# Projections and attention in one stage: tiles in three rounds, gates last, first maxima between the last gate tiles

## The chip, the cores and the metric

The kernel runs on one core of one Trainium2 chip. Times are microseconds on the device. The core has five engines with a queue each: PE (TensorE, matmuls; PEld its weight loads), DVE (VectorE), ACT (ScalarE), POOL (GpSimd) and SP (SyncE, which here only issues DMAs). They wait for each other by semaphores alone. The metric is the device time of one execution, given as the median of several.

## What is computed

Two residual blocks follow each other on 2048 tokens of width 1024: gated linear attention, then a block with attention and a convolution side by side. The change lies in the second.

```python
u = rms_norm(h, norm_w) * (1.0 + scale) + shift
p = u @ w_in                                   # 1024 -> 2816 columns
q, k, v = qk_heads(p, q_norm_w, k_norm_w)      # 8 query heads, 2 key heads, width 64
q = rope_2d(q, angles)
k = rope_2d(k, angles)
k_c, v_c = kv_heads(uc @ w_in[:, K_LO:V_HI], k_norm_w)     # 256 context keys
k_all = jnp.concatenate([k_c, k], axis=1)      # 2304 keys
v_all = jnp.concatenate([v_c, v], axis=1)
attn = attend_blocked(q, k_all, v_all) * jax.nn.silu(p[..., ZA_LO:ZA_HI])
conv = conformer_conv(p[..., GLU_LO:GLU_HI], ...) * jax.nn.silu(p[..., ZC_LO:ZC_HI])
out = jnp.concatenate([attn, conv], axis=-1) @ w_out
h = h + gate[:, None, :] * out
```

`attend_blocked` is a softmax over all 2304 keys for each query head. `conformer_conv` is a gated input, a depthwise convolution of 31 taps over the tokens, a layer norm, a swish and a pointwise product.

## The kernel before

Everything is float32; a product is made of three passes with the operands split into a high and a low part. The second block has three stages, each with its own buffers and with a barrier of all engines ahead of it (L1256, L1837, L2295): `projections`, `attention`, `output`. The first two belong to different phases, so the SBUF of `projections` is given back before that of `attention` is taken.

**Projections** (L1147). The 2048 tokens are four blocks of 512. For each block b, `NW = 22` tiles of 128 output columns are made, j = 0 to 21, block after block: 88 tiles, each 24 matmuls (L1421) into one of two banks, G[j % 2]. Tiles 0 to 7 are the convolution's input and its gate in turn, 8 to 12 the four pairs of query heads and the keys, 13 the values, 14 to 21 the eight gates `za` and `zc`. ACT reads a tile out of its bank (L1554 to L1576; a gate tile is read twice, once plain and once through a tanh), and the next but one tile may then be written. DVE makes from two reads the convolution's input (L1658) or a gate (L1709), which SP stores. What is kept between ACT and DVE lies in `ga` and `gt`, two slots each.

The heads go through a chain spread over the following tiles: squares summed over a head by PE (L1430), a root by ACT and DVE, spread back by PE (L1436), scaled by DVE (L1686), halves swapped by eight small DMAs of SP (`swap_q`, L1285), turned by DVE (`turn_q`, `add_turned_q`) and stored by SP to the scratch tensors `qt` and `kt` (`store_q`, L1291). In block b the chain ends in the first tile of block b + 1; the last block's ends after its last tile.

The convolution's 4 x 124 taps (each a multiply and add over 512 or, in the last block, 528 tokens, `tap`, L1618) run on DVE behind what each tile needs of it; `OWN` says how many go with each tile. What is left of a block's taps after its last tile runs with the first four tiles of the next.

**Attention** (L1732). 32 steps, one for each query head and block of 512 queries, eight heads over two groups of keys (g = 0, 1). A step has 18 key tiles, kt. For each: scores of 128 keys x 512 queries into one of three banks `att_bank_s` (L1970, L1971), an exponential by ACT (L2070) into `p_f`, and the sum of `p_f` pair by pair (POOL L1915, DVE L2135). The product with the values (`weigh`, L1945) comes in three groups of twelve matmuls, two in the step (at kt 9 and 14) and one in the next (at kt 2).

The exponential needs a row of maxima first, one value for each query, subtracted within the scores through row 65 of `q_b`. These maxima are taken one step ahead: 20 pieces (`piece`, L1930) of raw scores, 4 at a time between the key tiles of the step before, in four banks `att_bank_m`; DVE reduces each piece (L2121); after the last a small reduction (L2127), a transposition by PE (L1937) and a read by ACT (L2023) give the row. From the fifth piece on, PE waits before a pair of pieces for the reductions that free its banks:

```python
if p % 2 == 0:
    need(pe, mx_read, i * NP + max(p - MBANKS + 2, 0))
```

Step 0 has no step before it. Its pieces stand by themselves at the head of the stage, after the loads of Q and K (SP L1846, L1857), the rounding of K to its high part by ACT (`round_k`, L2012) and of Q (L2019). POOL makes the low part of K (L1901), 64 x 2304 values in one instruction, for each group. SP also loads V (L1861).

## Time and profile before

| | us |
|---|---|
| median of 3 runs (lowest, highest) | 2650.35 (2646.22, 2656.89) |
| the profiled execution, whole | 2648.54 |
| its span | 2646.5 |
| PE busy | 2470.5 (93%) |
| DVE busy | 1687.6 (64%) |
| ACT busy | 1008.9 (38%) |
| POOL busy | 694.6 (26%) |
| mean granted PE clock | 0.971 |

PE is the engine on the path nearly everywhere. The projections run from 1044.3 to 1574.3, the attention from there to about 2370, the output to the end. In the page's row of forty slices the granted clock stands at 0.8 to 0.9 of full speed except in one slice, the 25th, where it is 0.6: that slice holds the seam between projections and attention. A share of 1.00 is the full clock of 2.4 GHz, 0.50 is 1.2 GHz. The profiled execution lies between the lowest and the median run.

### The profile page before, as it was taken

The page shows a single profiled execution, that of the slowest core. Times are in us where ns is not written, and L with a number is a line of the kernel's source. Part 1 is how long each engine was busy: PE and PEld are TensorE (multiplying, and loading weights), DVE is VectorE, ACT ScalarE, POOL GpSimd, SP SyncE. Part 2 cuts the span into 40 slices and gives each one's busy share as a digit, 9 for nine tenths or more (in the row PEclk, how much of TensorE's full clock was granted, in tenths as well). Part 3 has the DMA queues.
Part 4 walks back from the last instruction along what each step waited for, and adds up shares of the span by engine and source line. Part 5 has one row for each costly group of instructions (what it writes and reads, how often), then busy time and mean ns, then how long its engine had stood idle before and what let it go on. Part 6 is the DMA issues. An engine that isn't in the chain of part 4 may idle for free. (4 is left out here: it accounts for less than half of the span.)

```text
span 2646.5 us, 33253 instructions
## 1 busy us (share of the span) xinstructions
PE 2470.5 (93%) x11265; PEld 1698.2 (64%) x11265; DVE 1687.6 (64%) x2746; ACT 1008.9 (38%) x1766; POOL 694.6 (26%) x313
## 2 busy tenths in 40 slices
PE   3898899999999998999999976999999999988997
PEld 1576677777777777777777763554555445546776
DVE  3236564654656461889997984777777777775664
ACT  4144444444345440332222123555445445451222
POOL 1233211111211100102000003677666566640000
PEclk8999999999999999999999996999999999998999
DMA  7964787388668747488767654111111110104334
GB/s 269 358 201 141 245 289 279 132 278 318 210 220 282 275 150 271 174 283 318 236 224 240 213 177 104 49 49 54 31 31 29 30 30 25 27 25 169 131 136 153
DMA packets 225145, 453.62 MB, mean 171 GB/s; under 512 B 23957, under 2 KB 82571, under 8 KB 224756
## 3 DMA queue, kind: packets, MB, share of 16 engines
q1 hardware_dynamic: 193960, 351.04, 39.3%
q10 hardware_dynamic: 31052, 100.87, 11.1%
q8 instruction: 76, 1.25, 0.2%
q14 instruction: 57, 0.47, 0.1%
HBM read 328.86 MB, written 109.35 MB: 166 GB/s over the span
## 5 line engine op out<-in xcount | busy, mean ns | idle before, releaser
L2121 DVE TENSOR_REDUCE att_mx<-att_bank_m 128x1 f32<-128x512 f32 (+1 forms) x640 | 365.2, 629 | 128.9 <-PE att_bank_m L1930 128.9
L2070 ACT ACTIVATE att_p_f<-att_bank_s 128x512 f32<-128x512 f32 x576 | 312.4, 599 | 284.1 <-PE att_bank_s L1971 276.0
L1915 POOL TENSOR_TENSOR att_den<-att_den,att_p_f 128x1024 f32<-128x1024 f32 x160 | 379.4, 2371 | 42.7 <-ACT att_p_f L2070 27.4
L1618 DVE SCALAR_TENSOR_TENSOR proj_conv_acc<-proj_conv_in,proj_conv_w,proj_conv_acc 128x512 f32<-128x512 f32 (+1 forms) x480 | 337.4, 772 | 0.0
L562 PE MATMUL gla_bank_g<-mid_a_hi,mid_w_hi 128*128 128x512 f32 x768 | 310.8, 405 | 2.0 <-POOL mid_w_lo L515 1.1
L562 PE MATMUL gla_bank_g<-mid_a_hi,mid_w_lo 128*128 128x512 f32 x768 | 300.8, 392 | 0.0
L562 PE MATMUL gla_bank_g<-mid_a_lo,mid_w_hi 128*128 128x512 f32 x768 | 300.1, 391 | 0.0
L1945 PE MATMUL att_bank_o<-att_p_f,att_v 128*64 128x512 f32 x1152 | 270.6, 605 | 0.0
L562 PEld LDWEIGHTS gla_bank_g<-mid_a_hi,mid_w_hi 128*128 128x128 f32 x768 | 144.9, 189 | 48.3 <-issue 18.5
L1945 PEld LDWEIGHTS att_bank_o<-att_p_f,att_v 128*64 128x64 f32 x1152 | 74.6, 137 | 146.0 <-issue 104.9
L562 PEld LDWEIGHTS gla_bank_g<-mid_a_hi,mid_w_lo 128*128 128x128 f32 x768 | 144.6, 188 | 31.5
L562 PEld LDWEIGHTS gla_bank_g<-mid_a_lo,mid_w_hi 128*128 128x128 f32 x768 | 145.0, 189 | 29.4 <-issue 1.4
L508 POOL TENSOR_TENSOR mid_w_lo<-first_w_raw,mid_w_hi 128x1024 fp32r<-128x1024 f32 x22 | 54.7, 2486 | 379.6 <-ACT mid_w_hi L736 379.6
L1421 PE MATMUL proj_bank_g<-mid_a_hi,mid_w_hi 128*128 128x512 f32 x352 | 140.5, 399 | 5.7 <-PEq L1256 5.7
L1421 PE MATMUL proj_bank_g<-proj_u_hi,mid_w_hi 128*128 128x512 f32 x352 | 139.5, 396 | 0.0
L1421 PE MATMUL proj_bank_g<-mid_a_lo,mid_w_hi 128*128 128x512 f32 x352 | 137.6, 391 | 0.0
L1421 PE MATMUL proj_bank_g<-mid_a_hi,mid_w_lo 128*128 128x512 f32 x352 | 137.5, 391 | 0.0
L1421 PE MATMUL proj_bank_g<-proj_u_lo,mid_w_hi 128*128 128x512 f32 x352 | 137.1, 389 | 0.0
L1421 PE MATMUL proj_bank_g<-proj_u_hi,mid_w_lo 128*128 128x512 f32 x352 | 136.9, 389 | 0.0
L1970 PE MATMUL att_bank_s<-att_q_a,end_k_a 128*128 128x512 f32 x288 | 130.6, 454 | 1.0 <-ACT att_q_b L2023 1.0
L1970 PE MATMUL att_bank_s<-att_q_a,att_k_a 128*128 128x512 f32 x288 | 128.8, 447 | 2.4 <-issue 2.0
L1915 POOL TENSOR_TENSOR att_den<-att_p_f 128x1024 f32<-128x1024 f32 x32 | 75.7, 2366 | 196.3 <-ACT att_p_f L2070 196.3
(404 smaller groups left out, 4753.7 us busy)
## 6 DMA issues: line engine op xcount, KB each, us to landing
mid_w_hi<-scratch_w_hi SPq DMA_DIRECT2D x100, 512.0 KB, 4.5
mid_w_lo<-scratch_w_lo SPq DMA_DIRECT2D x100, 512.0 KB, 6.1
mid_w_hi<-scratch_w_hi ACTq DMA_DIRECT2D x84, 512.0 KB, 3.9
mid_w_lo<-scratch_w_lo ACTq DMA_DIRECT2D x84, 512.0 KB, 5.0
scratch_w_hi<-mid_w_hi SPq DMA_DIRECT2D x54, 512.0 KB, 6.3
scratch_w_lo<-mid_w_lo SPq DMA_DIRECT2D x54, 512.0 KB, 7.1
mod_wslab<-in_ada_w SPq DMA_DIRECT2D x6, 2048.0 KB, 18.4
first_w_raw<-in_gla_w_in SPq DMA_DIRECT2D x24, 512.0 KB, 6.7
```

The source lines that it names most:

```text
L508: pool.tensor_tensor(w2_lo[:], w_raw[m % 2][:], w2_hi[:].bitcast(F32), ALU.subtract).then_inc(w2_rest, 1)
L562: last = pe.matmul(G[s % 2][:], w[:, k, :], a[:, k, :], start=(k == 0 and n == 0), stop=(k == KT - 1 and n == 2))
L1421: last = pe.matmul(G[j % 2][:], w[:, k, :], a[half][:, k, :], start=(k == 0 and n == 0), stop=(k == KT - 1 and n == 2))
L1618: dve.scalar_tensor_tensor(acc, src, conv_w[:, c, k:k + 1], acc, ALU.mult, ALU.add).then_inc(taps, 1)
L1915: pool.tensor_tensor(den[s][:], pair(0) if j == 1 else den[s][:], pair(j), ALU.add).then_inc(den_pool, 1)
L1945: last = pe.matmul(O[HD * half:HD * (half + 1), :], v[g][:, 2 * j + half, :], p_f[:, 2 * j + half, :], start=(j == 0), stop=(j == NPR - 1))
L1970: pe.matmul(S[kt % SBANKS][:], k_a[g][:, keys], q_a[s][:], start=True, stop=False)
L2070: act.activation(p_f[:, kt, :], S[kt % SBANKS][:], ACT.Exp, scale=float(HD) ** -0.5).then_inc(p_done, 1)
L2121: dve.reduce_max(mx[:, qt, n:n + 1], M[p % MBANKS][:, 0:min(TB, KEYS - TB * n)], AX_X).then_inc(mx_read, 1)
```

## The change

Projections and attention become one stage, `projections_and_attention`. `attention` no longer opens a block of its own: it returns for each engine a few pieces of code (`begin.sync`, `begin.tensor` and so on), which the projections' loops call at chosen tiles, and a `rest`, which holds the steps. No barrier stands between them, and the two `UNCONDITIONAL_BRANCH` rows go. Buffers of both live side by side, with attention's at fixed places (`attention_places`), and attention's banks are those of the projections under other names: scores in bank_q, bank_s and bank_g0, maxima in bank_n, bank_x, bank_y and bank_v, the output in bank_g1.

The 88 tiles are no longer dealt block by block but in three rounds, numbered through as t = 0 to 87:

- round 0: block 0 as before (t 0 to 21);
- round 1: block 1's convolution and heads, then block 2's convolution, then block 1's gates (t 22 to 51);
- round 2: block 2's heads, block 3's convolution, block 3's heads, block 2's gates, block 3's gates (t 52 to 87).

Each block's chain of heads follows at the same distance in tiles as before, with the keys first in the turning (`HEADS`), and ends two tiles earlier. The number of taps per tile is one list of 88 numbers; no tap is left for after the last tile. Stores of taps stand at seven named tiles. The rounding of block 3's input is done in the first four tiles of round 2.

From t = 80, block 3's first gate, on: at 80 SP loads Q 0, K of group 0 and Q 1, and ACT sets the row of ones; at 81 ACT rounds Q, at 82 K; from 83 PE issues four pieces after each tile; from 84 DVE reduces four pieces after the gate product of that tile and before its taps, with the last four after tile 87; V is loaded, now as one tensor for both groups, at 87. K of group 1 is loaded at the start of step 0, rounded at its key tile 9, and its low part is made on POOL between the adds of that step.

```diff
@@ the rounds and the taps of each tile
-    LATE = 4
-    OWN = [[7] * 7 + [6] * 3 + [5] * 2 + [4, 3, 3, 4, 4, 5]] * 2 + [[7] + [6] * 8 + [7] + [6] * 2 + [5] * 2 + [4] * 4] + [
-        [8, 8, 8, 7, 8, 7, 8, 7, 8, 7] + [7, 7, 6, 6, 6, 6, 5, 5]]
+    HEADS = (4, 0, 1, 2, 3)
+    CONV, HEAD, GATE = range(0, 8), range(8, 14), range(14, NW)
+    ROUNDS = (((0, CONV), (0, HEAD), (0, GATE)), ((1, CONV), (1, HEAD), (2, CONV), (1, GATE)),
+              ((2, HEAD), (3, CONV), (3, HEAD), (2, GATE), (3, GATE)))
+    TAPS_OF_TURN = [0, 0, 0, 0, 7, 7, 6, 5, 7, 6, 9, 4, 12, 12, 2, 7, 4, 5, 1, 3, 3, 4, 5, 7, 7, 1, 7, 7, 7, 7, 9, 8, 9, 4, 8, 8, 3, 7, 6, 5, 3, 3, 4, 4,
+                    4, 7, 7, 7, 7, 7, 7, 7, 7, 7, 7, 7, 7, 9, 4, 8, 7, 6, 4, 3, 4, 4, 5, 9, 9, 9, 9, 9, 3, 8, 6, 6, 3, 3, 3, 4, 4, 7, 7, 8, 5, 5, 4, 0]
+    STORE_TAPS = {14: (0, 0), 27: (0, 1), 36: (1, 0), 48: (1, 1), 57: (2, 0), 68: (2, 1), 76: (3, 0)}
@@ when a slot of ga and gt is free
+    def slot_free(act, glu, z_done, b, kind):
+
+        n = USERS.index((b, kind - kind % 2 if kind in CONV else kind))
+        if n >= 2:
+            b, kind = USERS[n - 2]
+            if kind in CONV:
+                act.wait_ge(glu, UP + b * 4 + kind // 2 + 1)
+            else:
+                act.wait_ge(z_done, UP + b * 8 + kind - GATE[0] + 1)
@@ SP
+                    if r == 2 and j == GATES_LAST:
+                        sp.wait_ge(proj, UP + TURN[NB - 1, GATE[0]])
...
+                        sp.wait_ge(q_stored[4], UP + 16 * NB)
+                        sp.wait_ge(q_stored[0], UP + 16)
+                        load_q_and_k()
+                    if r == 2 and j == GATES_LAST + 7:
+                        load_v()
@@ PE
+                    if r == 2 and j >= GATES_LAST + 3:
...
+                        first_maxima(4 * (j - GATES_LAST - 3))
+                pe.wait_ge(q_n, UP + NB * 5)
+                pe.wait_ge(evac, UP + NB * NW + 1)
+                rest()
@@ ACT
+                    if r == 2:
+                        if j == GATES_LAST:
+                            set_ones(0)
+                        if j == GATES_LAST + 1:
+                            round_q(0, 0)
+                        if j == GATES_LAST + 2:
+                            round_k(0)
+                rest()
@@ DVE
+                    if r == 2 and j == GATES_LAST + 3:
+                        split_first_q()
+                    if r == 2 and j >= GATES_LAST + 4:
+                        first_maxima(4 * (j - GATES_LAST - 4))
+                    next_taps(sum(TAPS_OF_TURN[:t]), TAPS_OF_TURN[t])
+                first_maxima(16)
+                first_column()
+                rest()
@@ attention, group 1's keys
-                for g in range(NKV):
-                    pool.wait_ge(k_hi_done, UP + g + 1)
-                    pool.tensor_tensor(k_b[g][0:HD, :], k_raw[g][0:HD, :], k_a[g][0:HD, :].bitcast(F32), ALU.subtract).then_inc(k_lo_done, 1)
+                if j == 5 and at_step(i, 0):
+                    rest_of_k(1)
+                if kt == 9 and at_step(i, 0):
+                    round_k(1)
+                if kt == 14 and at_step(i, 0):
+                    set_ones(1)
```

What now stands where, on the two engines of the seam. First PE, before: the end of the last projection tile, and the twenty pieces and the transposition ahead of step 0.

```order
L1421 MATMUL proj_bank_g<-proj_u_hi,mid_w_lo 128x512
L1257 UNCONDITIONAL_BRANCH
L1918 UNCONDITIONAL_BRANCH
L1930 MATMUL att_bank_m<-end_k_a,att_q_c 128x512 x4
L1930 MATMUL att_bank_m<-end_k_a,att_q_c 128x256
```

PE in the changed kernel: the last matmul of tile 87, the last four pieces, the transposition and the first scores of step 0.

```order
L1462 MATMUL proj_bank_g<-proj_u_hi,mid_w_lo 128x512
L2014 MATMUL proj_bank_n<-att_k_a,att_q_c 128x512
L2014 MATMUL proj_bank_x<-att_k_a,att_q_c 128x512
L2014 MATMUL proj_bank_y<-att_k_a,att_q_c 128x512
L2014 MATMUL proj_bank_v<-att_k_a,att_q_c 128x256
L2021 MATMUL proj_bank_n<-ident_sb,att_mz 65x128 x4
L2057 MATMUL proj_bank_q<-att_q_a,att_k_a 128x512
L2058 MATMUL proj_bank_q<-att_q_b,att_k_b 128x512
```

Sixteen of the twenty pieces now stand ahead of this, four after each of tiles 83 to 86, and nothing divides the last tile from the last pieces.

DVE before, from the last gate product on (`proj_zout` is the gate, `proj_conv_acc` a tap, `proj_qraw` and `proj_qsin` a head being turned):

```order
L1709 SCALAR_TENSOR_TENSOR proj_zout<-proj_gt,proj_ga 128x512
L1632 TENSOR_TENSOR proj_qraw<-proj_qraw,proj_qsin 128x512
L1618 SCALAR_TENSOR_TENSOR proj_conv_acc<-proj_conv_in,proj_conv_w,proj_conv_acc 128x528 x5
L1625 TENSOR_TENSOR proj_qraw<-proj_qraw,proj_cos 128x512
L1626 TENSOR_TENSOR proj_qsin<-proj_qsin,proj_sin 128x512
L1632 TENSOR_TENSOR proj_qraw<-proj_qraw,proj_qsin 128x512
L1257 UNCONDITIONAL_BRANCH
L2108 UNCONDITIONAL_BRANCH
L2114 TENSOR_TENSOR att_q_a<-att_q_raw,att_q_c 64x512
L2121 TENSOR_REDUCE att_mx<-att_bank_m 128x1 x20
L2127 TENSOR_REDUCE att_mz<-att_mx 128x4
```

DVE in the changed kernel, tiles 83 and 84:

```order
L1760 SCALAR_TENSOR_TENSOR proj_zout<-proj_gt,proj_ga 128x512
L2217 TENSOR_TENSOR att_q_a<-att_q_raw,att_q_c 64x512
L1279 SCALAR_TENSOR_TENSOR proj_conv_acc<-proj_conv_in,proj_conv_w,proj_conv_acc 128x528 x8
L1760 SCALAR_TENSOR_TENSOR proj_zout<-proj_gt,proj_ga 128x512
L2224 TENSOR_REDUCE att_mx<-proj_bank_n 128x1
L2224 TENSOR_REDUCE att_mx<-proj_bank_x 128x1
L2224 TENSOR_REDUCE att_mx<-proj_bank_y 128x1
L2224 TENSOR_REDUCE att_mx<-proj_bank_v 128x1
L1279 SCALAR_TENSOR_TENSOR proj_conv_acc<-proj_conv_in,proj_conv_w,proj_conv_acc 128x528 x5
```

The reductions stand behind the gate product of their tile and ahead of its taps; in tiles 85 and 86 the same follows with five and four taps, in tile 87 with eight reductions and none.

## Rows read from the trace of the kernel before

**Rows 1.** Windows by stage: busy us (instructions) by engine, granted clock, DMA share, GB/s.

```profile
core 0: us, PE busy (x) PEld busy (x) DVE busy (x) ACT busy (x) POOL busy (x), PEclk, DMA share, GB/s
...
1185.60:1574.30 388.70, 388.68 (x1645) 300.84 (x1643) 349.15 (x523) 86.42 (x143) 14.01 (x7) 1.00 0.70 239
...
1606.10:1620.40 14.30, 8.69 (x24) 3.55 (x24) 12.00 (x22) 3.04 (x3) 9.99 (x2) 0.50 0.87 167
1620.40:1638.30 17.90, 17.84 (x44) 8.87 (x44) 6.92 (x12) 5.97 (x10) 9.44 (x4) 0.51 0.04 15
```

**Rows 2.** Timeline at the seam: start, length, engine, line, what, idle before it and releaser.

```profile
1603.79 2.12 ACT L2012 ACTIVATE end_k_a<-att_k_raw 128x2304 fp32r<-128x2304 f32 x1 [0.88 <-DMA att_k_raw<-scratch_kt]
...
1606.16 1.22 PE L1930 MATMUL att_bank_m<-end_k_a,att_q_c 64*128 64x512 f32 x4 [31.89 <-ACT end_k_a L2012]
```

**Rows 3.** Timeline of ACT and DVE in the last two gate tiles.

```profile
1568.88 0.60 ACT L1575 ACTIVATE proj_ga<-proj_bank_g 128x512 f32<-128x512 f32 x1 [4.98 <-PE proj_bank_g L1421]
...
1573.56 0.68 DVE L1709 SCALAR_TENSOR_TENSOR proj_zout<-proj_gt,proj_ga 128x512 f32<-128x512 f32 x1
...
1574.32 0.60 ACT L1575 ACTIVATE proj_ga<-proj_bank_g 128x512 f32<-128x512 f32 x1 [4.35 <-PE proj_bank_g L1421]
1574.76 3.48 DVE L1618 SCALAR_TENSOR_TENSOR proj_conv_acc<-proj_conv_in,proj_conv_w,proj_conv_acc 128x528 f32<-128x528 f32 x5
1574.81 0.59 ACT L1576 ACTIVATE proj_gt<-proj_bank_g 128x512 f32<-128x512 f32 x1
```

**Rows 4.** DMA issues from 1575 to 1640: count, KB each, median us to landing.

```profile
att_k_raw<-scratch_kt SPq DMA_DIRECT2D x4, 576.0 KB, 9.3
att_v<-scratch_vtok SPq DMA_DIRECT2D x2, 576.0 KB, 15.5
```

**Rows 5.** Timeline in step 0: four pieces on PE and their reductions.

```profile
1641.70 0.73 PE L1930 MATMUL att_bank_m<-end_k_a,att_q_c 64*128 64x512 f32 x4
...
1642.23 2.22 DVE L2121 TENSOR_REDUCE att_mx<-att_bank_m 128x1 f32<-128x512 f32 x4 [0.52 <-PE att_bank_m L1930]
```

**Rows 6.** Timeline of steps 0 and 1; the L1970 rows here open steps 0, 1, 2.

```profile
1618.13 0.17 DVE L2127 TENSOR_REDUCE att_mz<-att_mx 128x4 f32<-128x20 f32 x1
...
1620.46 0.77 PE L1970 MATMUL att_bank_s<-att_q_a,end_k_a 128*128 128x512 f32 x1 [0.99 <-ACT att_q_b L2023]
...
1647.13 0.50 PE L1970 MATMUL att_bank_s<-att_q_a,end_k_a 128*128 128x512 f32 x1
...
1649.57 2.79 PE L1945 MATMUL att_bank_o<-att_p_f,att_v 128*64 128x512 f32 x12
...
1654.57 1.05 PE L1953 MATMUL att_bank_o<-end_ones,att_den 128*128 128x1 f32 x8
...
1656.51 0.60 PE L1960 MATMUL att_bank_o<-ident_sb,att_recip 128*128 128x128 f32 x4
...
1670.18 0.50 PE L1970 MATMUL att_bank_s<-att_q_a,end_k_a 128*128 128x512 f32 x1
```

**Rows 7.** Timeline of DVE's taps and POOL in block 1, and POOL at the seam.

```profile
1205.79 8.04 DVE L1618 SCALAR_TENSOR_TENSOR proj_conv_acc<-proj_conv_in,proj_conv_w,proj_conv_acc 128x512 f32<-128x512 f32 x12
...
1214.35 5.84 DVE L1618 SCALAR_TENSOR_TENSOR proj_conv_acc<-proj_conv_in,proj_conv_w,proj_conv_acc 128x512 f32<-128x512 f32 x4
...
1216.32 1.61 POOL L1248 TENSOR_TENSOR proj_hrs<-proj_hrs,proj_ht 128x512 f32<-128x512 f32 x1 [0.74 <-ACT proj_ht L1464]
...
1605.99 5.06 POOL L1901 TENSOR_TENSOR end_k_b<-att_k_raw,end_k_a 64x2304 fp32r<-64x2304 f32 x1 [12.53 <-ACT end_k_a L2012]
```

**Rows 8.** Timeline of PE round two short idle gaps in the first block.

```profile
278.10 1.09 PE L650 MATMUL gla_bank_t<-ident_sb,gla_on 128*128 128x128 f32 x8 [1.62 <-ACT gla_on L865]
...
308.96 0.47 PE L562 MATMUL gla_bank_g<-gla_y_hi,mid_w_hi 128*128 128x512 f32 x1 [2.14 <-POOL mid_w_lo L515]
...
310.23 0.63 PE L562 MATMUL gla_bank_g<-gla_y_hi,mid_w_lo 128*128 128x512 f32 x1
```

**Rows 9.** Window of 2 us after the second gap (columns as in Rows 1).

```profile
310.00:312.00 2.00, 2.00 (x7) 1.55 (x6) 1.24 (x2) 2.00 (x3) 0.00 (x0) 0.53 1.03 396
```

**Rows 10.** Timeline of SP's queue: the eight swaps of one head.

```profile
1560.63 6.10 SPq L1285 DMA_DIRECT2D proj_qsin<-proj_qraw  x8
```

More of the change, by code:

```diff
@@ L1 @@
+from collections import namedtuple
 from contextlib import ExitStack
@@ L1144, with projections_and_attention @@
 CONV_AT = TB + LAG
-def projections(nc, d, keep):
+def projections_and_attention(nc, d, keep):
     NW = 22
@@ new lines, in _ @@
+                    for c, jq in chains(t):
+                        if 18 <= jq < 23:
+                            add_turned_q(c, jq - 18)
+                    if r == 2 and j == GATES_LAST + 3:
[5 more added lines that the diff above has]
+                first_column()
+                rest()
@@ L1736, in attention @@
+def attention(nc, d, keep, ctx):
     NKT = KEYS // P
@@ new lines, in at_step, with need, pair, steps @@
+    def at_step(i, n):
+        return isinstance(i, int) and i == n
+    def need(eng, semaphore, n):
+        if isinstance(n, int) and n <= 0:
+            return
+        eng.wait_ge(semaphore, UP + n)
+    def pair(j):
+        return p_f[:, 2 * j:2 * j + 2, :]
+    def steps(eng, body):
+        last = GROUP_STEPS - 1
+        for g in range(NKV):
+            base = g * GROUP_STEPS
+            body(base, 0, g, g - 1 if g else None, g)
+            single = 2 if g else SINGLE
+            for n in range(1, single):
+                body(base + n, n % 2, g, g, g)
+            with eng.Fori(single // 2, GROUP_STEPS // 2 - 1) as it:
+                for s in range(2):
+                    body(it * 2 + (base + s), s, g, g, g)
+            body(base + last - 1, 0, g, g, g)
+            body(base + last, 1, g, g, g + 1 if g + 1 < NKV else None)
```

1519 lines of the change are left out of this document (771 added, 748 removed).

## The prediction

> **What bounds the kernel now.** I read first the windows by stage, then the timeline across the seam between projections and attention, then the granted clock round idle gaps of TensorE, and last what VectorE does in a gate tile. Through blocks 1 to 3 of the projections PE is busy for 388.68 of 388.70 us [rows 1]: there is nothing to win inside them, only something to lose, and VectorE has 349.15 us of work in the same time, 90%. Then PE stands idle for 31.89 us [rows 2], does the twenty first maxima in 14.3 us at half clock, waits for the row of maxima, and starts the scores of step 0 at 1620.46. The granted clock comes back to full only at about 1638.3 [rows 1]. The last tile's matmuls had ended at 1574.28 (the last row of ScalarE's read of a tile starts 0.04 us later, at 1574.32 [rows 3]). So 46.2 us lie between the last tile and step 0, and step 0 itself is slow.
>
> **What happens in the gap** [rows 2]: SP stores the last taps, all engines meet at a barrier, K and Q are loaded, ScalarE rounds K at 1603.79, and the first maximum starts at 1606.16. None of that needs the last gate tiles; it needs K, which is finished earlier in the new order.
>
> **Part 1, the barrier and the loads.** The load of K and Q moves to tile 80 of 88, the rounding of K to tile 82. From the end of tile 80 to the end of tile 83 are three tiles of 5.44 us (1568.88 to 1574.32 [rows 3]), 16.3 us. K is issued about 2.5 us after tile 79 ends (ScalarE's read, VectorE's gate product, the gate store ahead of it on SP) and so well before tile 80's end; the nearest price of its landing is 9.3 us [rows 4], where it had the rings almost to itself. Now weight pairs and gate stores run beside it, so I allow up to twice that. With 2.12 us of rounding [rows 2] that is 12 to 21 us against at least 16 of cover: a stall of 0 to 7 us (the issue's 2.5 us included), and I take 1. V goes out as one transfer of twice the width at the last tile; its two halves took 15.5 us [rows 4], and step 0 starts some 17 us after its issue, so I take nothing for it.
>
> **Part 2, the maxima between the last gate tiles.** PE has twenty pieces (a piece: one 128x512 or 128x256 block of raw scores for a maximum) in five groups of four, after tiles 83 to 87; a group costs PE 0.66 us (0.73 with its overlap [rows 5]). The first group finds four free banks. Each later group must wait until VectorE has reduced the group before. And VectorE's turn is written as: gate product of this tile, then the four reductions, then taps. The gate product waits for ScalarE, which needs 1.12 us after the tile (to the end of its second read, 1574.81 plus 0.59 [rows 3]). So after tiles 85 and 86 PE waits 1.16 + 0.60 (gate product, by the spacing of its row and the next two) + 2.22 (four reductions [rows 5]) + 0.4 (hand-over and last two pieces) = 4.4 us each. After tile 84 VectorE is late as well: turn 83 holds 0.60 + 0.69 + 8 taps of 0.69 (3.48 us for five [rows 3]) = 6.8 us against a tile and a group of 6.1, so 5.1 us. With 0.7 for the first group the tiles grow by 14.6 us. After tile 87: 1.16 + 0.60 + eight reductions 4.4 + the small one 0.17 + transpose, read of the row and start of the scores 1.6 (2.16 at half clock, 1618.30 to 1620.46 [rows 6]) = 8.0 us. In all 22.6 us in place of 46.2: **23.6 saved**.
>
> **Part 3, GpSimd's rest of K.** It is one instruction of 5.06 us [rows 7] and now falls among taps. Where GpSimd's adds of 1.61 us ran among taps, four taps took 5.84 us, while twelve without them had taken 8.04, so 2.7 for four [rows 7]: the taps lost 3.1 us to two such adds, nearly their whole length. If the 5.06 us fall into turns 82 or 83, VectorE reaches the reductions after tile 84 up to 5 us later and PE waits for it; if it starts only while VectorE reads PSUM, it costs nothing. Bounds 0 and 5; I take 4, since the instruction becomes ready in the middle of the taps. The Trainium skill ("SBUF — State Buffer", the engine side of the port section) says that the pair of ports is an exclusive lock and the loser blocks for the whole instruction, which would make it 5.06 rather than 4, and the time 2633; the loss of 3.1 us under two adds of 1.61 agrees with it.
>
> **Part 4, the clock.** PE idled 1.62 us at 276 and stayed at full clock; it idled 2.14 us and then, from 310.23 on, ran eight matmuls at 0.63 instead of 0.40 us, with a granted clock of 0.53, about half, which is 1.2 GHz against 2.4 [rows 8, 9]. Eight starts at 0.43 apart in place of 0.23 cost 1.7 us. Here PE idles 3 us or more after each of tiles 84 to 87 before two pieces of 0.3 us. Four falls: **6.8 us given back**. Bounds: nothing, and a clock that stays down (rivals). The Trainium skill ("TensorE: Matmul & The Clock Gate", HAM oscillation) warns only of idle gaps longer than three of these four; by that one fall would remain, 5.1 us better than my sum. The row with 2.14 us speaks against it, so it is a rival and not the forecast.
>
> **Part 5, step 0.** It took 26.67 us (1620.46 to 1647.13), step 1 took 23.05; step 1 also does the weighing, the sum and the spreading left from the step before, 2.79 + 1.05 + 0.60 us [rows 6] (both steps do their own weighing beside that). At full clock step 0 would be about 18.7: **8.0 saved**. Against it: K of group 1 is now loaded, rounded (2.12 us on ScalarE) and split (5.06 on GpSimd) within step 0, where GpSimd's six adds come before VectorE's last sums. GpSimd ends some 2.5 us later than the sums want, and the pieces and the sum of step 1 wait. 0 to 4 us, I take 1.5.
>
> **Part 6, the dealing of tiles and taps.** The same 88 tiles, 496 taps and weight loads in another order. By the durations in rows 4, VectorE's work per turn in rounds 1 and 2 is 4.7 to 6.8 us, 355 in all against 389 of PE [rows 1]; the heaviest are tiles 67 to 71, nine taps each, 6.2, beside longer turns of PE (they hold a head's sum). A tile's read needs the product of two users ago, so VectorE may lag by over 10 us before PE notices. Cost 0; above, up to 15 (rival). Taps that ran after the last tile lie before it now: no gain by itself, they ended inside the gap.
>
> **The sum**: 23.6 - 1 - 4 - 6.8 + 8.0 - 1.5 = 18.3 us, from the profiled execution's 2648.54 (span 2646.5 and 2 outside) to 2630.2. The median of three runs was 1.8 above that, so **2632**. The attention steps after step 1 and the output are untouched.
>
> **Rivals.**
> - **The clock holds in the short gaps**, or GpSimd slips in for nothing: 5.1 or 4 us more, 2623 to 2628, centre 2625. For it: the idle time is cut by two pieces. Against: the 2.14 us row. 0.20.
> - **The clock stays down** from tile 85 through step 0: three tiles cost 16.3 more in place of 6.8 and step 0 saves nothing: 23.6 - 1 - 4 - 16.3 - 1.5 = 0.8, so 2650. For it: before, 8.69 us of work in 14.3 us at 0.50 did not bring the clock back [rows 1]. Against: here full tiles of 5.4 us stand between the gaps, and the 2.14 us gap was followed by dense work and the clock was whole again 3.4 us after its fall. 0.09.
> - **The projections lose what they had**: SP spends 6.10 us on one head's eight swaps [rows 10] against turns of 6.07, and in tiles 77 and 78 it now also stores a head and a gate (0.6 each), so swaps, gate stores and with them VectorE slip; or chain steps hold PE up where two blocks overlap. 12 us, 2644. 0.13.
> - **K comes late and takes the clock with it** (slower): K shares the rings with the last weight pairs. If it lands after 35 us rather than 9.3, PE stands 25 us after tile 83, and after such a gap it runs the last four tiles at half clock (21.8 more): 23.6 - 25 - 21.8 - 1.5 = -24.7, so 2675. It becomes slower than before as soon as a stall is long enough to keep the clock down to step 0, and by over 0.5% from a stall of 14 us. The weight loads end with tile 87's, issued after tile 83, which speaks against it. 0.08.
>
> **How the numbers follow.** The forecast, 0.50, has a range of its own of 2623 to 2641. About 0.5%, 13 us, is what a measurement here can tell from no change: below 2637 is faster, above 2663 slower. Faster: 0.39 of the forecast, 0.20, and 0.01 of the third rival: 0.60. Slower: 0.08. Same: 0.32. For 8 in 10 the range runs from 2619, where the clock holds and nothing else costs, to 2655, which takes in the clock that stays down and most of the third rival, and leaves out the last.
>
> **What would show it.** In the profile after: no idle stretch above 10 us before attention; the first maxima starting between gate tiles, with PE waiting for the reductions 4 to 5 us at a time; granted clock dipping to about half for some 3 us after each; step 0 of 19 to 21 us; PE busy without a break through tiles 22 to 83. I am wrong if PE waits for ScalarE or VectorE earlier than tile 84, if the wait after tile 83 is for K, or if the attention steps after the first are not 23.6 us long.

## The result: 0.8% slower, and the profile after

| | before | after |
|---|---|---|
| median (lowest, highest), 6 runs each | 2652.55 (2646.22, 2656.89) | 2671.87 (2667.06, 2678.10) |
| span of the profiled execution | 2646.5 | 2664.9 |
| PE busy | 2470.5 | 2485.8 |
| mean granted PE clock | 0.971 | 0.970 |

The ratio is 1.0079, with a 95% interval of 1.0065 to 1.0093. The forecast was 2632, in a range of 2619 to 2655. The two spans differ by 18.4 us, the medians by 19.3.

First what PE waited for. These are rows of PE in the timeline after (start, length, engine, line, what; in brackets the idle time before it and what ended it). L2014 is a piece, L2021 the transposition, L2057 a score. The rows at 1628.58, 1654.53 and 1688.37 open steps 0, 1 and 2.

```profile
1285.54 0.47 PE L1478 MATMUL proj_bank_q<-proj_qrs_parts,proj_head_spread 42*128 42x512 f32 x1 [3.28 <-issue]
...
1565.75 0.76 PE L2014 MATMUL proj_bank_n<-att_k_a,att_q_c 64*128 64x512 f32 x1 [5.45 <-ACT att_k_a L2101]
...
1584.97 0.58 PE L2014 MATMUL proj_bank_n<-att_k_a,att_q_c 64*128 64x256 f32 x1 [11.13 <-DVE att_mx L2224]
...
1596.91 0.79 PE L2014 MATMUL proj_bank_n<-att_k_a,att_q_c 64*128 64x512 f32 x1 [2.90 <-DVE att_mx L2224]
...
1609.68 0.50 PE L2014 MATMUL proj_bank_n<-att_k_a,att_q_c 64*128 64x512 f32 x1 [2.90 <-DVE att_mx L2224]
...
1623.15 0.50 PE L2014 MATMUL proj_bank_n<-att_k_a,att_q_c 64*128 64x512 f32 x1 [3.17 <-DVE att_mx L2224]
...
1628.58 0.77 PE L2057 MATMUL proj_bank_q<-att_q_a,att_k_a 128*128 128x512 f32 x1 [0.99 <-ACT att_q_b L2112]
...
1654.53 0.50 PE L2057 MATMUL proj_bank_q<-att_q_a,att_k_a 128*128 128x512 f32 x1
...
1665.66 0.58 PE L2014 MATMUL proj_bank_n<-att_k_a,att_q_c 64*128 64x256 f32 x1 [4.29 <-DVE att_mx L2224]
...
1688.37 0.50 PE L2057 MATMUL proj_bank_q<-att_q_a,att_k_a 128*128 128x512 f32 x1
```

Before, step 0 started at 1620.46 [rows 6]; now it starts at 1628.58. The one wait of 31.89 us [rows 2] is gone, and seven smaller ones of 2.90 to 11.13 us have come: one at tile 37, five at the seam, one in step 1. The windows after, of the seam (from tile 83's end), of step 0, of the first and of the second part of step 1, show the granted clock round them:

```profile
core 0: us, PE busy (x) PEld busy (x) DVE busy (x) ACT busy (x) POOL busy (x), PEclk, DMA share, GB/s
1560.30:1628.60 68.30, 38.21 (x121) 26.60 (x121) 40.06 (x60) 8.54 (x13) 5.38 (x2) 0.72 0.35 115
1628.60:1654.50 25.90, 25.90 (x84) 13.21 (x84) 11.53 (x21) 14.46 (x20) 15.49 (x6) 0.69 0.26 57
1654.50:1665.60 11.10, 6.87 (x29) 3.03 (x28) 7.05 (x7) 4.92 (x10) 8.09 (x4) 0.97 0.39 115
1665.60:1688.40 22.80, 22.34 (x81) 11.76 (x81) 14.08 (x25) 8.70 (x15) 10.46 (x5) 0.71 0.06 19
```

**Where the 18.4 us are.** Both traces, laid side by side tile by tile and step by step:

| stretch | before | after | difference | forecast |
|---|---|---|---|---|
| start of the first tile | 1044.31 | 1045.42 | +1.1 | 0 |
| tiles, without the seam's waits | 529.97 | 536.64 | +6.7 | 0 |
| seam beyond the tiles' own 5.44 us each | 46.2 | 46.5 | +0.3 | -11.8 |
| step 0 | 26.67 | 25.95 | -0.7 | -8.0 |
| step 1 | 23.05 | 33.84 | +10.8 | +1.5 |
| all that follows | | | +0.2 | 0 |

The second row is the way to the end of tile 83 (1560.30) plus four tiles of 5.44, which is the way from one tile to the next where nothing waits. Of its 6.7 us, 4.9 arise at tiles 37 and 38, at the wait of 3.28 us in the first row of the timeline and the half clock behind it.

Then the engine that PE waited for. In the seam after, ACT waits 5.77 us for K, with its read of tile 82 queued behind; DVE waits for the store of an earlier gate, its gate product takes 3.71 us in place of 0.69 beside POOL's 5.10, and fifteen taps stand between it and the first reduction:

```profile
1563.37 2.12 ACT L2101 ACTIVATE att_k_a<-att_k_raw 128x2304 fp32r<-128x2304 f32 x1 [5.77 <-DMA att_k_raw<-scratch_kt]
...
1565.82 5.10 POOL L1981 TENSOR_TENSOR att_k_b<-att_k_raw,att_k_a 64x2304 fp32r<-64x2304 f32 x1
...
1567.76 3.71 DVE L1760 SCALAR_TENSOR_TENSOR proj_zout<-proj_gt,proj_ga 128x512 f32<-128x512 f32 x1 [6.63 <-DMA scratch_za<-proj_zout]
1571.40 4.83 DVE L1279 SCALAR_TENSOR_TENSOR proj_conv_acc<-proj_conv_in,proj_conv_w,proj_conv_acc 128x528 f32<-128x528 f32 x7
1576.16 0.68 DVE L1760 SCALAR_TENSOR_TENSOR proj_zout<-proj_gt,proj_ga 128x512 f32<-128x512 f32 x1
1576.87 0.69 DVE L2217 TENSOR_TENSOR att_q_a<-att_q_raw,att_q_c 64x512 fp32r<-64x512 f32 x1
1577.59 5.53 DVE L1279 SCALAR_TENSOR_TENSOR proj_conv_acc<-proj_conv_in,proj_conv_w,proj_conv_acc 128x528 f32<-128x528 f32 x8
1583.03 0.69 DVE L1760 SCALAR_TENSOR_TENSOR proj_zout<-proj_gt,proj_ga 128x512 f32<-128x512 f32 x1
1583.63 0.68 DVE L2224 TENSOR_REDUCE att_mx<-proj_bank_n 128x1 f32<-128x512 f32 x1
```

And in steps 0 and 1 the low part of group 1's keys stands on POOL ahead of its last two adds, DVE's sums wait for these, and the reductions of step 1 stand behind the sums:

```profile
1648.45 5.10 POOL L1981 TENSOR_TENSOR att_k_b<-att_k_raw,att_k_a 64x2304 fp32r<-64x2304 f32 x1 [4.09 <-ACT att_p_f L2169]
1653.52 4.90 POOL L2000 TENSOR_TENSOR att_den<-att_den,att_p_f 128x1024 f32<-128x1024 f32 x2
...
1658.45 1.23 DVE L2238 TENSOR_TENSOR att_den<-att_den,att_p_f 128x1024 f32<-128x1024 f32 x1 [6.39 <-POOL att_den L2000]
...
1664.33 0.68 DVE L2224 TENSOR_REDUCE att_mx<-proj_bank_n 128x1 f32<-128x512 f32 x1
```

### The profile page after: what moved, and what is told of

It is laid out like the page before. It is cut to its first block and busy times, and to the rows that moved or that the text cites. A ratio compares the mean times of both kernels' runs of the same rounds, so it can differ in the third digit from the quotient of the medians.

```text
span 2664.9 us, 33266 instructions
## 1 busy us (share of the span) xinstructions
PE 2485.8 (93%) x11265; PEld 1706.3 (64%) x11265; DVE 1692.1 (63%) x2746; ACT 1009.3 (38%) x1766; POOL 698.3 (26%) x313
## 5 line engine op out<-in xcount | busy, mean ns | idle before, releaser
L2029 PE MATMUL proj_bank_g<-att_p_f,att_v 128*64 128x512 f32 x1152 | 271.7, 607 | 0.0
L2224 DVE TENSOR_REDUCE att_mx<-proj_bank_n 128x1 f32<-128x512 f32 (+1 forms) x160 | 101.8, 636 | 123.1 <-PE proj_bank_x L2014 79.5
L2169 ACT ACTIVATE att_p_f<-proj_bank_q 128x512 f32<-128x512 f32 x192 | 114.4, 596 | 150.2 <-PE proj_bank_q L2058 147.2
L2029 PEld LDWEIGHTS proj_bank_g<-att_p_f,att_v 128*64 128x64 f32 x1152 | 75.1, 138 | 147.4 <-issue 106.3
L2169 ACT ACTIVATE att_p_f<-proj_bank_s 128x512 f32<-128x512 f32 x192 | 114.8, 598 | 103.0 <-PE proj_bank_s L2058 101.3
L2169 ACT ACTIVATE att_p_f<-proj_bank_g 128x512 f32<-128x512 f32 x192 | 115.7, 602 | 35.5 <-PE proj_bank_g L2058 32.0
```

Of the source, the lines that this page charges most:

```text
L2029: last = pe.matmul(O[HD * half:HD * (half + 1), :], v[g][:, 2 * j + half, :], p_f[:, 2 * j + half, :], start=(j == 0), stop=(j == NPR - 1))
L2169: act.activation(p_f[:, kt, :], S[kt % SBANKS][:], ACT.Exp, scale=float(HD) ** -0.5).then_inc(p_done, 1)
L2224: dve.reduce_max(mx[:, qt, n:n + 1], M[p % MBANKS][:, 0:min(TB, KEYS - TB * n)], AX_X).then_inc(mx_read, 1)
```

## Experiments

Each kernel is the changed one with the edit named, unless another base is given. The interval behind a ratio is the 95% interval against the kernel before. Edits are cut to their core. In the profiles the first tile starts anywhere between 1044 and 1055, and the stretch from the start of the last step to the end takes 306.9 to 310.0 us, though no edit touches either; so stretches are compared, and not clock times or whole spans. The changed kernel's own interval is 1.0065 to 1.0093. Those of e1, e8, e10, e11 and e12 lie below it. Those of e2, e3, e4, e5 and e7 overlap with it: what they gain by the medians, 3 to 6 us, is not clear of noise, and what is read from them is read from their traces. The same holds for e10 and e11 against e5, their base.

### First: four suspects, one edit each

**e1, reductions ahead of the gate product** in the last four tiles.

```diff
+                    if r == 2 and j >= GATES_LAST + 4:
+                        first_maxima(4 * (j - GATES_LAST - 4))
+                    if t == NB * NW - 1:
+                        first_maxima(16)
+                        first_column()
                     if kind in GATE:
...
-                    if r == 2 and j >= GATES_LAST + 4:
-                        first_maxima(4 * (j - GATES_LAST - 4))
```

> Edit: in the last four gate tiles VectorE reduces the pieces of the tile before AHEAD of its gate product, in the last one all eight and the small reduction. Theory 1 (the order in VectorE's turn is what TensorE waits for, and the waits are what pull its clock down): the waits of 2.9, 2.9 and 3.2 us after tiles 85 to 87 go, tiles 86 and 87 run at full clock, 6.1 us from one to the next in place of 11.9 and 12.8, and the way from tile 87's start to step 0 shrinks from 17.0 to about 11. Together 17 us less than the changed kernel: 2655. The wait of 11.1 us after tile 84 stays. Theory 2 (the short pieces themselves take the clock down): only the waits go, tiles still take 7 us and more, 10 us less: 2662.

Measured: 2657.58, ratio 1.0020 (1.0006 to 1.0034), 14 us less than the changed kernel. The wait after tile 84 stayed (10.58 us). Of the waits of 2.90 us after tiles 85 and 86 nothing is left behind 85 and 0.70 us behind 86. Windows of tiles 85, 86 and 87 in e1, each with the pieces behind it: the clock comes back within tile 85, 5.5 us after the wait, and stays to the end of tile 87.

```profile
1585.80:1593.70 7.90, 7.90 (x30) 5.93 (x28) 5.36 (x9) 0.48 (x1) 0.00 (x0) 0.78 0.10 35
1593.80:1601.10 7.30, 6.60 (x29) 4.77 (x28) 6.59 (x11) 1.59 (x4) 0.00 (x0) 1.00 0.10 36
1601.10:1607.00 5.90, 5.90 (x27) 4.65 (x28) 5.17 (x9) 0.12 (x1) 0.00 (x0) 1.00 0.69 201
```

So theory 1: with the same short pieces and no long wait before them, the clock stays up. The tail kept a wait of 4.80 us for the copy of Q 0, which SP issues behind the last stores; that is more than the 3 us by which e1 fell short of 17.

**e2, group 1's low part on VectorE** behind the row of maxima of step 1.

```diff
-                if j == 5 and at_step(i, 0):
-                    rest_of_k(1)
+                if kt == 14 and at_step(i, 0):
+                    dve.wait_ge(k_hi_done, UP + 2)
+                    dve.tensor_tensor(k_b[1][0:HD, :], k_raw[1][0:HD, :], k_a[1][0:HD, :].bitcast(F32), ALU.subtract)
```

> Edit: the low part of group 1's keys is made by VectorE after the row of maxima of step 1, not by GpSimd ahead of its fifth add in step 0. Theory 1 (GpSimd's 5.10 us push its last two adds, VectorE's sums behind them and so the reductions of step 1): step 1 falls from 33.8 to 23.5 us, the wait of 4.3 us in it and the half clock behind it go: 10 us less, 2662. Theory 2 (step 1 is slow because TensorE comes out of step 0 late and cold, and VectorE pays its own 2.7 us for the subtraction): step 1 stays above 30 us, under 3 us less, 2669 or more.

Measured: 2665.75, ratio 1.0052 (1.0035 to 1.0068), 6 us less by the medians. Step 1 took 26.99 us in place of 33.84, between the two theories. The wait of 4.29 us is gone, but two of 0.28 and 0.18 us are left, and about 3 us later the clock is at half. Step 1 of e2, PE:

```profile
1670.14 0.50 PE L2012 MATMUL proj_bank_y<-att_k_a,att_q_c 64*128 64x512 f32 x1 [0.28 <-DVE att_mx L2222]
...
1670.82 1.02 PE L2035 MATMUL proj_bank_g<-ones_sb,att_den 128*128 128x1 f32 x8 [0.18 <-DVE att_k_raw L2244]
```

**e3, twelve taps of block 1 later.**

```diff
-... 7, 7, 7, 7, 9, 8, 9, 4, 8, 8, 3, 7, 6, 5, 3, 3, 4, 4, 4, 7, ...
+... 7, 7, 6, 6, 7, 7, 7, 4, 5, 6, 3, 7, 6, 7, 5, 5, 6, 6, 6, 7, ...
```

> Edit: 12 taps of block 1 are moved from tiles 28 to 35 to tiles 39 to 44, nothing else. Theory 1 (VectorE is more than a tile behind when the roots of block 1's heads are due at tile 36, and TensorE waits 3.3 us for them): the wait of 3.28 us at tile 37 and the half clock after it go, tile 66 starts 6 us earlier, 2666. Theory 2 (the chain is late because of ScalarE's loads of tables and GpSimd's adds): the wait stays at 2 to 3 us, no change, 2671.

Measured: 2667.66, ratio 1.0061 (1.0044 to 1.0078), 4 us less by the medians. The wait of 3.28 us is not in the trace any more, and tile 66 starts 401.4 us after tile 0, where it was 407.2 in the changed kernel and 400.7 before. Theory 1: the loss inside the projections is one place where DVE was behind with its taps when the heads' roots were due.

**e4, K rounded behind tile 83's read** in place of tile 82's.

```diff
-                        if j == GATES_LAST + 2:
+                        if j == GATES_LAST + 3:
                             round_k(0)
```

> Edit: ScalarE rounds K one tile later, behind its reads of tile 83. Theory 1 (ScalarE, which waits 5.8 us for K's landing ahead of its read of tile 82, makes VectorE late, and this is most of the wait of 11.1 us after tile 84): that wait falls to 3 to 5 us, the wait for K after tile 83 stays at about 5.5, 7 us less, 2665. Theory 2 (VectorE is late because the store of tile 80's gate lands only after the loads of K and Q ahead of it in the queue): VectorE still waits until about 1567 for it, TensorE's wait stays above 9 us, under 2 us less.

Measured: 2669.21, ratio 1.0063 (1.0045 to 1.0080), 3 us less by the medians, but in the trace the way from tile 83's end to step 0 is no shorter (69.4 us, 68.3 in the changed kernel). ACT reads tiles 82 and 83 by 1563.8, and DVE still waits, for the store:

```profile
1570.18 3.99 DVE L1760 SCALAR_TENSOR_TENSOR proj_zout<-proj_gt,proj_ga 128x512 f32<-128x512 f32 x1 [6.79 <-DMA scratch_za<-proj_zout]
```

PE's wait after tile 84 is 9.84 us. So theory 2, as far as the wait goes. The DMA issues of the changed kernel between 1549 and 1556 (count, KB each, us to landing) show that the gate store was not late alone: everything issued then was. Gate stores issued between 1575 and 1600, with no loads beside them, took 2.1 us.

```profile
att_k_raw<-scratch_kt SPq DMA_DIRECT2D x2, 576.0 KB, 12.2
mid_w_hi<-scratch_w_hi ACTq DMA_DIRECT2D x2, 512.0 KB, 12.9
mid_w_lo<-scratch_w_lo ACTq DMA_DIRECT2D x1, 512.0 KB, 15.3
att_q_raw<-scratch_qt SPq DMA_DIRECT2D x2, 128.0 KB, 14.2
scratch_za<-proj_zout SPq DMA_DIRECT2D x1, 256.0 KB, 15.2
...
```

### Second: the loads themselves, and where the pieces stand

**e5, K and Q 0 early.** Their raw forms get a place that is free since tile 57; most of K is loaded at tile 72, its last 512 columns at tile 80.

```diff
+                    if t == EARLY:
...
+                        load_early()
                     if r == 2 and j == GATES_LAST:
...
-                        load_q_and_k()
+                        load_last_k()
+                    if r == 2 and j == GATES_LAST + 4:
+                        load_second_q()
```

> Edit: the raw K of group 0 and Q 0 get places that are free since tile 57; Q 0 and K's first 1792 columns are loaded at tile 72, K's last 512 at tile 80, Q 1 at tile 84. Rounding and pieces stay where they are. Theory 1 (the big loads at tile 80 are the root: they land late, hold ScalarE 5.8 us ahead of tile 82's read, and the gate stores queue behind them, so VectorE is late): the wait of 5.45 us after tile 83 goes, and the wait after tile 84 falls from 11.1 to about 5 us, the price on record; 11 us less, 2661. Theory 2 (the gate stores are late because of weights and head stores, which stay): only the 5.45 us go, the wait after tile 84 stays above 9: 2666.

Measured: 2668.80, ratio 1.0070 (1.0047 to 1.0093), 3 us less by the medians; from tile 83's end to step 0 it is 62.2 us in place of 68.3. Both theories missed the main thing. The wait of 5.45 us is gone, DVE waits for no store from tile 81 on, and still PE waits longer after tile 84 than in the changed kernel, 11.96 us in place of 11.13. DVE and POOL of e5, and PE after tile 84:

```profile
1564.71 9.81 DVE L1280 SCALAR_TENSOR_TENSOR proj_conv_acc<-proj_conv_in,proj_conv_w,proj_conv_acc 128x528 f32<-128x528 f32 x7
...
1563.86 6.01 POOL L1998 TENSOR_TENSOR att_k_b<-att_k_raw,att_k_a 64x2304 fp32r<-64x2304 f32 x1
...
1583.25 0.58 PE L2031 MATMUL proj_bank_n<-att_k_a,att_q_c 64*128 64x256 f32 x1 [11.96 <-DVE att_mx L2241]
```

Seven taps took 9.81 us where seven took 4.84 just ahead of them. DVE has no idle time from 1555 to the reductions. What the loads had cost, the lock of POOL and the taps cost as well: two causes for one lateness, and taking one away shows the other.

**e8, all pieces after tile 87**, none between the tiles.

```diff
-                    if r == 2 and j >= GATES_LAST + 3:
-                        first_maxima(4 * (j - GATES_LAST - 3))
+                for first in range(0, 20, 4):
+                    first_maxima(first)
```

> Edit: all twenty pieces and reductions after tile 87, none between the gate tiles; K's load and rounding stay at tiles 80 and 82. Theory 1 (each short wait between tiles costs its length and the clock of the tile behind it, so that hiding pieces there costs more than it saves): tiles 84 to 87 run 5.44 us from one to the next, then VectorE finishes its late taps and the twenty pieces take some 14 us at half clock; the way from tile 83's end to step 0 is 37 to 50 us in place of 68.3: 19 to 31 less, 2641 to 2652. Theory 2 (the plan's price is right, pieces between tiles are cheaper than after them): 68 us or more, no gain.

Measured: 2651.36, ratio 0.9996 (0.9982 to 1.0009), 20 us less than the changed kernel and the same as before. From tile 83's end to step 0 it is 48.2 us in place of 68.3. Theory 1: as they stood, the pieces between the tiles cost 20 us. DVE's lateness shows here too. PE of e8 after tile 87:

```profile
1600.33 0.58 PE L2012 MATMUL proj_bank_n<-att_k_a,att_q_c 64*128 64x256 f32 x1 [11.65 <-DVE att_mx L2222]
```

**e7, group 1's keys rounded at the end of step 0, low part in step 2.** The outputs of steps 0 to 2 get their own place, since they had lain over the raw keys.

```diff
-                if kt == 9 and at_step(i, 0):
+                if kt == 15 and at_step(i, 0):
                     round_k(1)
...
+            if at_step(i, 2):
+                pool.wait_ge(den_dve, UP + i * DVE_ADDS)
+                rest_of_k(1)
```

> Edit: only group 1's keys: rounded at key tile 15 of step 0, low part on GpSimd at the head of step 2, where it has nothing else; the outputs of steps 0 to 2 get a place of their own for that. Theory 1 (the low part of group 1 is the whole loss of step 1): step 1 takes 23 to 24 us in place of 33.8, step 2 at most 1 us more than 23.6; 10 us less, 2662. Theory 2 (a step 1 that follows a cold step 0 loses its clock at the smallest wait, as with the low part on VectorE, where it took 27.0): 27 us again, 2665.

Measured: 2669.06, ratio 1.0073 (1.0050 to 1.0096). Step 1 took 26.72 us: theory 2 in its number, but not in its cause. ACT's rounding of 2.1 us stood ahead of the exponential of key tile 16 of step 0. That exponential frees the bank into which PE writes its second scores of step 1, and PE waited 2.03 us for it.

**e12, the same with the rounding at key tile 13 of step 1.**

> Edit: the changed kernel with group 1's keys rounded at key tile 13 of step 1, their low part on GpSimd at the head of step 2. Theory 1 (in the kernel with the rounding at key tile 15 of step 0, ScalarE's 2.1 us stood between two exponentials and cost a wait of 2.0 us and the clock; with it away nothing else of group 1 costs): step 1 takes 23 to 24 us in place of 33.8, step 2 up to 24.5; 10 us less than the changed kernel, 2661. Theory 2 (the load of group 1's keys at step 0 or the cold step 0 is the cost): step 1 above 26 us, 2665.

Measured: 2663.68, ratio 1.0047 (1.0032 to 1.0061), 8 us less than the changed kernel. Step 1 took 23.05 us, as before the change, though step 0 ahead of it was as slow as ever (25.95). Step 3 took 24.10 in place of the 23.02 before. Theory 1, and it says what e2's and e7's 27 us were: each had left a wait in step 1, with half clock behind it, and without one the step takes 23.

### Third: VectorE at the seam, on the base of e5

**e10, GpSimd's low part only after tile 87.**

```diff
         pool.memset(mz[:], 0.0).then_inc(cleared, 1)
+        pool.wait_ge(proj, tiles)
         rest_of_k(0)
```

> Edit: the kernel with K early (e5), and in it GpSimd's low part of K only after tile 87. Theory 1 (GpSimd's 6 us block VectorE's taps, seven of which took 9.81 us in place of 4.84): seven taps take 4.84 us, the wait of 11.96 us after tile 84 falls to 7, and the 8.6 us between tile 87 and step 0 cover GpSimd: 5 us less than e5, 2664. Theory 2 (the slow taps are slow for another reason, or the low part ends too late for step 0): the wait stays or comes back as a wait ahead of step 0, no change, 2669.

Measured: 2660.55, ratio 1.0037 (1.0019 to 1.0056), 8 us less than e5. The seven taps of that turn, and PE's wait after tile 84:

```profile
1562.42 4.84 DVE L1280 SCALAR_TENSOR_TENSOR proj_conv_acc<-proj_conv_in,proj_conv_w,proj_conv_acc 128x528 f32<-128x528 f32 x7
...
1575.99 0.58 PE L2032 MATMUL proj_bank_n<-att_k_a,att_q_c 64*128 64x256 f32 x1 [6.05 <-DVE att_mx L2242]
```

Theory 1, and by more than expected. A part came back behind tile 87, where the gate product now lies beside POOL's 5.04 us, takes 4.46, and PE waits 6.93 us in place of 3.17.

**e11, ten taps of tiles 81 to 83 moved** to tiles 61 to 66 and 76 to 79.

```diff
-... 7, 6, 4, 3, 4, 4, 5, 9, ... 3, 3, 3, 4, 4, 7, 7, 8, 5, ...
+... 7, 7, 5, 5, 5, 5, 6, 9, ... 4, 4, 3, 5, 4, 4, 4, 4, 5, ...
```

> Edit: the kernel with K early (e5), and in it ten taps of tiles 81 to 83 moved to tiles 61 to 66 and 76 to 79. Theory 1 (VectorE comes a tile late and with more work than a tile has, so the first reductions wait for the taps ahead of them, and TensorE for the reductions): the wait of 11.96 us after tile 84 falls by the ten taps' 6.9 us to 5, 2662. Theory 2 (the lateness comes from the stores and swaps, and ten taps earlier make VectorE later before): the wait stays above 9, under 3 us less.

Measured: 2662.61, ratio 1.0035 (1.0023 to 1.0047), 6 us less than e5. DVE's four taps beside POOL, and PE's wait after tile 84:

```profile
1557.93 7.77 DVE L1280 SCALAR_TENSOR_TENSOR proj_conv_acc<-proj_conv_in,proj_conv_w,proj_conv_acc 128x528 f32<-128x528 f32 x4
...
1571.72 0.58 PE L2031 MATMUL proj_bank_n<-att_k_a,att_q_c 64*128 64x256 f32 x1 [5.52 <-DVE att_mx L2241]
```

The wait fell by 6.4 us, where ten taps are 6.9. The trace bears out theory 1. The four taps still took 4.96 us more than four take without POOL (2.81 in the same trace).

### Fourth: all together

**e6**: e1, e3, e5 and e7, the pieces one tile earlier (after tiles 82 to 86, none after 87) and with them the rounding of Q 0 (tile 80) and K (tile 81), the copies of Q 0 at tile 83, V at tile 86.

```diff
-                    if r == 2 and j >= GATES_LAST + 3:
+                    if r == 2 and GATES_LAST + 2 <= j < GATES_LAST + 7:
...
-                        first_maxima(4 * (j - GATES_LAST - 3))
+                        first_maxima(4 * (j - GATES_LAST - 2))
```

> Edits together: reductions ahead of the gate product, taps of block 1 later, K early with its rounding behind tile 81, the pieces after tiles 82 to 86 (none after 87), the copies of Q 0 at tile 83, V at tile 86, group 1's keys rounded at the end of step 0 and their low part on GpSimd at the head of step 2. Theory 1 (every wait found so far is one of order, and without waits the clock stays up): no wait over 1 us from tile 0 to step 0, step 0 starts some 2 us after tile 87 and takes 18.7 us at full clock, step 1 takes 23: 66 us less than the changed kernel, 2606. Theory 2 (VectorE has no room: its taps, gates and twenty reductions are 49 us against 47 of TensorE in the last tiles, and GpSimd blocks it for 5): TensorE waits 5 to 10 us for reductions and loses the clock in the last tiles: 2620 to 2630.

Measured: 2633.41, ratio 0.9940 (0.9916 to 0.9964): faster than before by 0.6%. That is 27 us above theory 1 and 3 us above theory 2's range. PE still waited 6.17 us for the reductions after tile 83 and 1.79 for K, so theory 2 holds for the seam. Step 1 took 28.29 us, since PE waited 2.04 us in it as in e7. But from tile 84 to step 0 PE idles at most 1.22 us at a time, and step 0 ran at full clock. Windows of e6, step 0 and the two parts of the start of step 1:

```profile
1601.80:1621.10 19.30, 18.99 (x84) 9.63 (x84) 11.93 (x22) 9.56 (x18) 14.21 (x6) 1.00 0.59 143
1621.20:1624.00 2.80, 0.76 (x4) 0.32 (x3) 1.32 (x2) 2.77 (x3) 0.00 (x0) 0.97 0.43 98
1624.00:1630.00 6.00, 6.00 (x16) 2.60 (x18) 4.40 (x6) 2.07 (x4) 0.00 (x0) 0.50 0.67 216
```

Step 0 took 19.39 us at 1.00, against 25.95 at 0.69 after and 26.67 before.

**e9**: e6 with e11's ten taps, the rounding of e12, K's last columns one tile earlier, and ACT's read of the first row ahead of its rounding of Q 1.

> Edits: the kernel with all edits (2633), with ten taps of tiles 81 to 83 moved to tiles 61 to 66 and 76 to 79, K's last 512 columns loaded one tile earlier, group 1's keys rounded at key tile 13 of step 1 in place of 15 of step 0, and ScalarE's read of the first row ahead of its rounding of Q 1. Theory 1 (what is left are three waits of order: 6.17 us for reductions after tile 83, 1.79 for K after tile 82, 2.04 for an exponential behind the rounding in step 1 with the half clock after it): the first falls under 1 us, the second under 0.5, step 1 takes 23 to 24 us in place of 28.3; 6 + 3 + 1.5 + 5 = 15 us less, 2618. Theory 2 (VectorE is full wherever the taps go, and a step 1 near a wait keeps its clock down): 2628 or more.

Measured: 2625.13, ratio 0.9894 (0.9876 to 0.9911): 1.1% faster than before, 47 us less than the changed kernel, and between the two theories (2618, 2628 or more). Step 0 took 19.37 and step 1 23.03, as theory 1 had it, and the wait for K fell from 1.79 to 0.96 us. The wait after tile 83, which theory 1 had under 1 us, stayed at 6.44 us: POOL's low part blocked DVE's four taps to 7.77 us, as in e11. Step 3 took 27.33 us. PE in step 3 of e9, and its windows behind these rows:

```profile
1677.15 0.50 PE L2065 MATMUL proj_bank_y<-att_k_a,att_q_c 64*128 64x512 f32 x1 [0.59 <-DVE att_mx L2276]
...
1677.83 1.02 PE L2088 MATMUL proj_bank_g<-ones_sb,att_den 128*128 128x1 f32 x8 [0.18 <-DVE again_o_first L2298]
```

```profile
1678.00:1681.00 3.00, 3.00 (x18) 2.67 (x18) 2.42 (x6) 1.09 (x2) 2.86 (x2) 0.84 0.01 3
1681.00:1684.00 3.00, 3.00 (x9) 1.20 (x10) 1.25 (x4) 2.25 (x3) 2.86 (x2) 0.50 0.20 46
1684.00:1687.00 3.00, 3.00 (x10) 0.90 (x8) 1.20 (x3) 0.00 (x0) 2.86 (x2) 0.52 0.00 0
```

## Why the prediction was wrong, point by point

The forecast said 18.3 us saved, the trace says 18.4 lost, a miss of 36.7: 12.1 in the seam, 9.3 in step 1, 7.3 in step 0, 7.8 ahead of the seam, 0.2 behind. The direction failed, and not by one term: VectorE's lateness, group 1's keys, the clock at step 0 and the dealing were each priced too low. The 12.1 of the seam are 4.9 ahead of tile 84, 4.0 after it, 0.8 after tiles 85 and 86, 0.6 in the tail and 1.8 of clock.

- **Part 1, the loads: mis-sized.** 1 us was taken within bounds of 0 to 7; 5.45 was measured. K took 12.2 us to land, within the "up to twice 9.3" allowed, but SP, busy with swaps and the stores of heads and gates, issued it at 1548.92, 10.4 us after tile 79's end (1538.5) and not 2.5. The bound of 7 was luck: from tile 79's end the cover is four tiles, 21.8 us, against 2.5 + 18.6 + 2.1, so by its own premises the stall was at most 1.4. What was left out is the other side of a load: six transfers of 1.7 MB in all, put into the busiest stretch, made a gate store land after 15.2 us, and DVE waits for that store. That the loads made it late is shown as far as this goes: in e5, with most of them earlier, DVE waits for no store from tile 81 on.
- **Part 2, the waits between tiles: right in kind, the first one wrong.** Forecast after tiles 84, 85, 86: 5.1, 4.4 and 4.4, hand-over and last pieces included; with Part 3's 4 us the first is 9.1. Measured, from a tile's last matmul to the next tile's first: 13.1, 4.8 and 4.8. The tail after tile 87: 8.0 against 8.6. The step that failed is DVE's lateness at tile 84. It was worked out from turn 83 alone, as if DVE stood level with PE at its start. Part 6 says that DVE may lag by over 10 us before PE notices, and calls that free. It was, until the reductions, for which PE waits at once, were put into that queue. e5, e10 and e11 show the two halves of it: 5 us by POOL's lock, 6.4 by ten taps.
- **Part 3, POOL blocks the taps: right, one row misread.** Forecast 4, bounds 0 and 5. In the changed kernel it cost 3.0 (a gate product of 3.71 in place of 0.69), because DVE was waiting for the store during POOL's first 2 us; in e5, 5.0. The Trainium skill ("SBUF — State Buffer", SBUF: two separate sides) says that the loser blocks for the whole instruction; by that, e11's four taps should lose nearly all of POOL's 5.68 us; they took 7.77 us in place of 2.81, 4.96 more, and agree. The same price was then missed on group 1's low part. And the twelve taps of 8.04 us [rows 7] did not run without POOL, as the prediction says; before has this row beside their last ones:

```profile
1210.50 5.08 POOL L1248 TENSOR_TENSOR proj_hrs<-proj_ht,proj_hms 128x512 f32<-128x512 f32 x1 [116.14 <-ACT proj_hms L1464]
```

  There the taps lost nothing, and it was POOL's instruction that took 5.08 us, where others of its kind take 1.28 to 1.61. So either engine can be the one that loses.
- **Part 4, the clock in the gaps: nearly right.** Forecast 6.8 for four falls. Tiles 84 to 87 took 6.94, 7.12, 7.96 and 8.38 us, 8.6 over four tiles of 5.44. The first of the four falls stands behind the wait for K, which the sum did not have as one.
- **Part 5, step 0: the sum was right, the condition was not.** "At full clock 18.7" is 19.4 in e6 and e9. (Its own subtraction, 23.05 less 4.44, gives 18.6.) But in the changed kernel PE idles 3.17, 1.64 and 0.99 us just ahead of step 0, the gap of 2.14 us [rows 8] was the row that said what this does, and 8.0 us were booked all the same. Part 4 priced falls behind tiles 84 to 86 and 87 and then let step 0 start warm.
- **Part 5, group 1's keys: the largest single miss.** "0 to 4, I take 1.5" was 10.8. The path was named (GpSimd's adds, VectorE's sums, the pieces of step 1) but priced as a delay of 2.5 us. POOL's 5.10 us shift its last adds by all of 5.10, DVE waits 6.39, its fold takes 2.71 in place of 0.69 beside POOL, PE waits 4.29, and the 22.80 us behind that run at a mean granted clock of 0.71. e12 gives back the whole 10.8.
- **Part 6, the dealing: wrong.** Cost 0, rival 12; measured 6.7. By e3, 5.8 of them are one wait behind too many taps, 3.28 us and the clock behind it. The rival named SP's swaps or the chain's steps, at 12 us; it was the chain. The matmul that waits (L1478) reads the heads' roots. ACT had done its first part of them at 1275.6, and DVE, six taps before it, took up its own 6.3 us later:

```profile
1281.89 0.67 DVE L1727 SCALAR_TENSOR_TENSOR proj_qt<-proj_bank_s,proj_qrs 10x512 f32<-10x512 f32 x1
```

  The durations that this part takes from rows 4 are those of rows 3. The 1.1 us at the start stand in no relation to the change that these runs can show: the code ahead of the first tile is the same in all profiles, and it starts between 1044 and 1055.

The rival nearest in time (K late, 2675) came true in its first words only: the stall was 5.45 us and not 25. The last four tiles ran at half clock in part, the first of them behind the wait for K and the others behind the waits for VectorE.

What stays open: why the same wait costs the clock in one run and not in another (below), and whether moving POOL's low part out of the taps would take e9's last 6.44 us. It was not tried.

## What to carry to other kernels

Before a consumer that PE waits for is put into an engine's queue, work out how late that engine runs there, over the last several turns and not from the one turn: slack that cost nothing becomes the wait. What is moved into that queue goes ahead of what can wait (e1, 14 us), and the optional work leaves the last turns (e11). A step taken from idle time has three prices: its own duration, what it blocks (another engine's instructions, a transfer queue, an engine's order), and the clock that may be lost behind a wait that it makes. In step 1 the third was the largest: of 10.8 us lost, PE waited 4.7.
